# 80 gathered tokens instead of 48, every second chunk of expert rows in plain fp32, rows by 512 KB in eight slots

## The reference, cut to what matters

```
qry = (hc @ w_query).reshape(-1, PEER_HEADS, 2, PEER_HALF)
...
act = jax.nn.gelu(jnp.einsum('cd,chkd->chk', hc, expert_u[idx]))
return jnp.einsum('chk,chkd->cd', gate * act, expert_v[idx])
```

## Time and profile before

| what | us |
|---|---|
| median of three runs | 2206.61 |
| the profiled execution | 2206.82 |
| its span | 2205.1 |
| TensorE busy | 2182.6 |
| DVE busy | 1657.7 |
| ACT busy | 1216.1 |
| GpSimd busy | 688.0 |

### The profile page before, as it was taken

The page is one execution under the profiler, slowest core; times in us unless marked ns, Lnnn a source line. Parts: engine busy times, 40 slices in busy tenths (PEclk is TensorE's granted clock), DMA queues, the critical chain, the costliest instruction groups (busy, mean ns, idle before and its releaser), DMA issues.

```text
span 2205.1 us, 55760 instructions
## 1 busy us (share of the span) xinstructions
PE 2182.6 (99%) x16578; PEld 2138.2 (97%) x16578; DVE 1657.7 (75%) x3045; ACT 1216.1 (55%) x2220; POOL 688.0 (31%) x516
## 2 busy tenths in 40 slices
PE   9999999999999999999999999999999999999998
PEld 8999899999999999999999999999999999999997
DVE  8788778886766767888886444467788887888887
ACT  6445366667455444555555444454565565555664
POOL 0321100002011000788888888500454122111120
PEclk9999999999999999999999999999999999999999
DMA  7887756666556555777777888698899998788885
GB/s 241 288 292 246 240 185 213 203 213 220 183 190 207 175 165 185 187 182 183 189 178 183 194 186 182 161 333 282 278 315 300 304 316 299 274 293 299 297 284 188
DMA packets 337994, 514.37 MB, mean 233 GB/s; under 512 B 87276, under 2 KB 126564, under 8 KB 337772
## 3 DMA queue, kind: packets, MB, share of 16 engines
q1 hardware_dynamic: 263244, 427.59, 60.0%
q0 software_dynamic: 58016, 71.54, 13.0%
q10 hardware_dynamic: 16640, 14.16, 2.0%
HBM read 487.87 MB, written 25.24 MB: 233 GB/s over the span
## 4 chain that ended last, share of the span: by engine, by line
PE 75%; DMA 1%; DVE 1%; ACT 0%; issue 0%; SPq 0%; DVEq 0%; ACTq 0%
PE ps L2173 18%; PE ps L314 15%; PE ps L317 15%; PE ps L313 15%; PE ps L2177 10%; DMA raw<-expert_v 0%; DMA raw<-weights 0%; PE ps L2197 0%; PE ps L1400 0%; ACT hi L296 0%; DVE x L2154 0%; DVE lo L301 0%; PE ps L2206 0%; DVE x L2095 0%; DVE whl L2034 0%
## 5 line engine op out<-in xcount | busy, mean ns | idle before, releaser
L301 DVE TENSOR_TENSOR lo<-raw,hi 128x512 fp32r<-128x512 f32 x1504 | 1027.8, 695 | 462.9 <-ACT hi L296 435.1
L296 ACT CAST hi<-raw 128x512 fp32r<-128x512 f32 x1504 | 924.5, 620 | 720.7 <-PE ps L317 443.0
L313 PE MATMUL ps<-h_hi,hi 128*128 128x264 f32 (+1 forms) x3200 | 821.4, 286 | 2.7 <-DVE h_lo L954 2.7
L314 PE MATMUL ps<-h_lo,hi 128*128 128x264 f32 (+1 forms) x3200 | 820.2, 286 | 0.0
L313 PEld LDWEIGHTS ps<-h_hi,hi 128*128 128x128 f32 x3200 | 601.9, 188 | 10.2 <-issue 6.1
L314 PEld LDWEIGHTS ps<-h_lo,hi 128*128 128x128 f32 x3200 | 602.3, 188 | 0.0
L317 PE MATMUL ps<-h_hi,lo 128*128 128x264 f32 (+1 forms) x3200 | 523.4, 285 | 2.1 <-DVE lo L301 1.9
L1732 POOL DMA_INDIRECT w_spill<-chosen,widx x256 | 442.2, 1727 | 265.1 <-DVE widx L1956 187.0
L2173 PE MATMUL ps<-whl,hi 128*128 128x432 f32 x2048 | 489.7, 361 | 1.9 <-ACT half_sum L1817 1.2
L317 PEld LDWEIGHTS ps<-h_hi,lo 128*128 128x128 f32 x3200 | 444.4, 188 | 3.8 <-DVE lo L301 3.5
L2173 PEld LDWEIGHTS ps<-whl,hi 128*128 128x128 f32 x2048 | 348.8, 190 | 10.6 <-issue 1.7
(11 more groups left out here) (300 smaller groups left out, 1787.9 us busy)
## 6 DMA issues: line engine op xcount, KB each, us to landing
raw<-u_tiles SPq DMA_DIRECT2D x512, 256.0 KB
raw<-expert_v SPq DMA_DIRECT2D x512, 256.0 KB
raw<-weights SPq DMA_DIRECT2D x480, 256.0 KB
w_spill<-zeros ACTq DMA_DIRECT2D x16, 864.0 KB, 6.0
wld<-w_spill SPq DMA_DIRECT2D x32, 432.0 KB, 4.4
qb<-q_spill POOLq DMA_DIRECT2D x8, 512.0 KB, 6.3
w_spill<-chosen,widx POOLq DMA_INDIRECT x256
u_spill<-ust SPq DMA_DIRECT2D x128, 24.0 KB
```

What stands on the lines that cost most here:

```text
L296: nc.scalar.copy(hi[k % SPLIT][:], raw_quarter(k)).then_inc(hi_done, 1)
L301: nc.vector.tensor_tensor(lo[k % SPLIT][:], raw_quarter(k), hi[k % SPLIT][:].bitcast(F32), ALU.subtract).then_inc(lo_done, 1)
L313: pe.matmul(out, a, rhs[0][:, first + j, 0:n], start=start and j == 0, stop=False)
L314: pe.matmul(out, a, rhs[1][:, first + j, 0:n], start=False, stop=False)
```

## The change

The gathered tokens become 80, in groups of 16 and 64, so the dense columns fall from 216 to 184. DVE makes five additions per iteration of eight chunks (ADDS: in places k = 1, 2, 3, 5, 6; none in the first iteration of the first half, six in its iterations 8 to 12). Ten words are gathered first, then two after each row from row 2 on. Odd chunks, but for the first and the last of them, are native: TensorE multiplies their rows as loaded, in plain fp32, with W in plain fp32 (`plain`), and no engine splits them; `credit` lets the counters of splits pass over them. Rows come as whole chunks of 512 KB into eight slots; a slot is free when a split chunk's two parts are made, or when TensorE is through a native chunk. Chunks 4 to 7 wait for chunks 0 to 3, and the last spill of u now stands behind the load of chunk 7. TensorE's loop covers eight chunks; the loops of ACT and DVE are written out.

```
-GROUPS = (16, 32)
+GROUPS = (16, 64)
+NATIVE = (1, 3, 5, 7)
+SLOTS = 8
...
+    raw_v = place("raw_v", at["W"], [P, SLOTS - RAW, HALF, P])
+    wld = place("wld", at["raw_v"], [P, 3, 4, TD])
...
-    LATE_ADDS = [(0, 2, 4, 6), (0, 2, 4, 6), (0, 2, 4, 6), (0, 2, 4)]
-    BOUNDS = (0, 1, FIRST, 8, LATE)
-    assert 3 * (LATE - 1) + sum(len(a) for a in LATE_ADDS) == TG and 3 * (NK // 8) == TG and GROUPS == (16, 32)
+    BOUNDS = (1, 3, 6, 9)
+    FIVE, SIX = (1, 2, 3, 5, 6), (1, 2, 3, 5, 6, 7)
+    ADDS = [[()] + 7 * [FIVE] + 4 * [SIX] + [SIX, FIVE, FIVE, (0, 1, 2, 3, 4)], 15 * [FIVE] + [(0, 1, 2, 3, 4)]]
...
+    def column(n):
+
+        turn, m = n % TG // TURN, n % TURN
+        return GROUPS[0] + (TURN - 1) * turn + m if m < TURN - 1 else turn
...
+    def native(m):
+
+        return m % 8 in NATIVE and m not in (1, 2 * NK - 1)
...
+    def expert_slot(s):
+
+        return raw[:, s] if s < RAW else raw_v[:, s - RAW]
...
+    def expert_in(s):
+
+        return raw_in[s % RAW][s // RAW]
...
+    def credit(q):
+
+        return 3 if q % 2 and native(q // 2 + 1) else 1
+
+    def expert_hi(act, q):
+        wait_expert(act, q)
+        act.wait_ge(mm_done, 2 * C0 + q + 1)
+        nc.scalar.copy(hi[q % SPLIT][:], expert_quarter(q)).then_inc(hi_done, credit(q))
+
+    def expert_lo(dve, q):
+        dve.wait_ge(hi_done, 2 * C0 + q + 2 * RAW + 1)
+        dve.wait_ge(mm_done, 2 * C0 + q + 1)
+        nc.vector.tensor_tensor(lo[q % SPLIT][:], expert_quarter(q), hi[q % SPLIT][:].bitcast(F32),
+                                ALU.subtract).then_inc(lo_done, credit(q))
...
+            for i in range(NK // 8):
+                if p == 0 and i in BOUNDS:
+                    between(0, i, None)
                 for k in range(8):
-                    half(1, 0, k)
-                with eng.Fori(1, LATE) as i:
-                    for k in range(8):
-                        half(1, i, k)
-            for i in range(LATE, NK // 8):
-                for k in range(8):
-                    if p == 0 or i < NK // 8 - 1 or k < 6:
-                        half(p, i, k)
-                    elif k == 6:
-                        half(p, i, k, 1)
+                    m = NK * p + 8 * i + k
+                    for q in (2 * m + AHEAD, 2 * m + AHEAD + 1):
+                        if q < 4 * NK and split_chunk(q // 2):
+                            split(eng, q)
+                    if k % 2 == 0 and m + 2 < 2 * NK:
+                        w_part(m + 2)
+                    between(p, i, k)
...
+    def w_chunks(c):
+
+        return 2 if split_chunk(c + 1) else 1
...
-        load_half(sp, C0 + RAW, 0, expert_v[0, RAW])
+        def load_expert(p, i, s):
+            m = NK * p + 8 * i + s
+            first = isinstance(i, int) and p == 0 and i == 0
+            back = m - (RAW if first else SLOTS)
+            if native(back if isinstance(i, int) else s + SLOTS):
+                sp.wait_ge(mm_done, 2 * (C0 + back) + 2 + SPLIT)
+            else:
+                sp.wait_ge(hi_done, 2 * (C0 + back) + 2 + 2 * RAW)
+                sp.wait_ge(lo_done, 2 * (C0 + back) + 2 + 2 * RAW)
+            sp.dma_start(expert_slot(s).rearrange("p a b -> p (a b)"), expert_v[p, 8 * i + s]).then_inc(expert_in(s), 16)
+        for s in range(RAW, SLOTS):
+            load_expert(0, 0, s)
         spill(PAIR_U - 1, 1)
...
+        load_expert(0, 1, 0)
+        load_expert(0, 1, 1)
         sp.wait_ge(w_mul, UP_CHUNKS + 4)
         cells_in(UP_CHUNKS + 1, 1)
-        stream(2, 3)
+        for s in range(2, SLOTS):
+            load_expert(0, 1, s)
...
+        with sp.Fori(0, NK // 8) as i:
+            for s in range(SLOTS):
+                load_expert(1, i, s)
...
+        for n in range(FIRST_WORDS):
             gather_u(n)
-        words = WORD_TURNS[1]
+        words = FIRST_WORDS
...
+            n = w_chunks(c)
+            nc.scalar.copy(whl[c // 2 % 2][:, 0:n, 0], W[:, c % NK:c % NK + n, :]).then_inc(whi_done, 2)
...
+        def add_rows(n):
+            j, b = column(n), n % 3
+            g = 0 if j < GROUPS[0] else 1
+            dve.wait_ge(gat_in[b], 16 * (n // 3) + 16)
             dve.wait_ge(gat_used, n + 1)
-            nc.vector.scalar_tensor_tensor(out=gacc[:, g], in0=gat[b][:], scalar=gw[:, bass.ds(j, 1)],
+            nc.vector.scalar_tensor_tensor(out=gacc[:, g], in0=gat[b][:], scalar=gw[:, j:j + 1],
...
+                weigh_rows(BOUNDS.index(i))
...
+            if (i, k) in ADD_AT[p]:
+                n = TG * p + ADD_AT[p][i, k]
+                if n == TG:
                     dve.wait_ge(gacc_zero, 2)
-                add_rows(1 - m // 2, TG + 3 * i + m, column(i, m), m, i + TG // 3)
-            if p == 1 and static and i == LATE + 1 and k % 4 == 0:
+                add_rows(n)
...
+        def plain(p, i, k, r, stop):
+            if isinstance(i, int) and not p and not i and k < RAW:
+                pe.wait_ge(raw_in[k][r], 16 * PAIR_U + 16)
+            elif r == 0:
+                pe.wait_ge(expert_in(k), 16 * (PAIR_U + 1 + NK // SLOTS * p + (k >= RAW)) + 16 * i)
+            for j in range(QT):
+                m = pe.matmul(ps[:, bank(QT * r + j), 0:TD], expert_slot(k)[:, QT * r + j],
+                              W[:, 8 * i + k if isinstance(i, int) else bass.ds(8 * i + k, 1), :],
+                              start=False, stop=stop, skip_group_check=True)
+            m.then_inc(mm_done, 1)
+
+        def quarter(p, i, k, r, stop=False):
+            if native(NK * p + 8 * i + k if isinstance(i, int) else k + SLOTS):
+                plain(p, i, k, r, stop)
+            else:
+                first = isinstance(i, int) and i == 0 and k == 0
+                f(NK * p + 8 * i + k, k, r, first, stop, p == 1 and first)
         for p in range(2):
+            for k in range(8):
+                for r in range(2):
+                    quarter(p, 0, k, r)
+            with pe.Fori(1, NK // 8 - 1) as i:
+                for k in range(8):
+                    for r in range(2):
+                        quarter(p, i, k, r)
...
```

More of the change, by code:

```diff
@@ L116, in program @@
     sums = place("sums", at["wsum"], [P, 2, TT, PH])
-    gch = place("gch", at["sums"], [P, 3, TG])
-    gw = place("gw", at["gch"], [P, TG])
+    gw = place("gw", at["sums"], [P, TG])
     gu = place("gu", at["gw"], [P, TG])
@@ new lines, in program @@
+    ADDS = [[()] + 7 * [FIVE] + 4 * [SIX] + [SIX, FIVE, FIVE, (0, 1, 2, 3, 4)], 15 * [FIVE] + [(0, 1, 2, 3, 4)]]
+    TURN = TG // (NK // 8)
+    assert all(sum(len(a) for a in adds) == TG for adds in ADDS) and GROUPS == (NK // 8, (TURN - 1) * NK // 8)
+    ADD_AT = [{k: sum(len(a) for a in adds[:i]) + n for i in range(NK // 8) for n, k in enumerate([(i, k) for k in adds[i]])}
+              for adds in ADDS]
+    G_FIRST = [sum(GROUPS[:g]) for g in range(len(GROUPS))]
+    WORD_TURNS = [-(-sum(len(a) for a in ADDS[0][:i]) // TURN) * TURN for i in BOUNDS] + [TG]
@@ L1583, in gather_rows @@
     def gather_rows(n):
-        j = column(n % TG // 3, n % 3)
+        j = column(n)
         index = gidx[:, 1 + n // TG, j:j + 1]
@@ L1590, in halves @@
     def halves(eng, w_part, split, between, after_pass):
[L1592 to L1598, removed]
-        for p in range(2):
[L1600 to L1604, removed]
-                        for k in range(8):
-                            half(0, i, k)
-                between(0, None, None)
-            else:
-                for k in range(8):
-                    half(1, 0, k)
-                with eng.Fori(1, LATE) as i:
-                    for k in range(8):
-                        half(1, i, k)
-            for i in range(LATE, NK // 8):
-                for k in range(8):
-                    if p == 0 or i < NK // 8 - 1 or k < 6:
-                        half(p, i, k)
-                    elif k == 6:
-                        half(p, i, k, 1)
+        for p in range(2):
+            for i in range(NK // 8):
+                if p == 0 and i in BOUNDS:
+                    between(0, i, None)
+                for k in range(8):
+                    m = NK * p + 8 * i + k
[5 more added lines that the diff above has]
+                    between(p, i, k)
             after_pass(p)
-    def chunk(i, k):
-        n = 8 * i + k
-        return bass.ds(n % NK if isinstance(i, int) else n, 2)
+    def w_chunks(c):
+        return 2 if split_chunk(c + 1) else 1
     def experts_sync(sp):
@@ L1747, in gather_u @@
         def gather_u(n):
-            j, batch = column(n // 3, n % 3), max(b for b in range(4) if n >= WORD_TURNS[b])
+            j, batch = column(n), max(b for b in range(4) if n >= WORD_TURNS[b])
             nc.gpsimd.indirect_dma_start(gu[:, j:j + 1], None, u_rows,
```

115 lines of the change are left out of this document (46 added, 69 removed).

## The result

The change made the kernel slower by 0.28%: 2212.86 us (median of 20 runs, 2207.35 to 2219.07) against 2206.06 (median of 20, 2203.27 to 2209.92), ratio 1.0028, 95% interval 1.0021 to 1.0036. That is just over the 0.2% that can be told from no change. The forecast was 2198.5 us and faster; 2212.86 lies inside its range of 2186 to 2216, but on the other side of the kernel before. The profiled execution of the changed kernel took 2210.11 us with a span of 2208.3.

A forecast was written before the change was run, and what follows sets the result against it. The prediction took TensorE, busy for 99% of the span, to bound the kernel. Its terms -25.3, -2, +11, +7 and +1 summed to -8.3 us, from 2206.8 to 2198.5 us, range 2186 to 2216.

The forecast's parts named there:

- Part 1: TensorE's work per chunk: split chunks fall to 2.226 us, plain ones take 2.48, against 2.45 before; -25.3 us.
- Parts 2 and 5: Work off ACT and DVE, costed at nothing; buffer turns in six-addition iterations fit, last additions closer to the ends, +1 us.
- plain products at 0.457 ns: Rival on TensorE: plain products go at the rate of rounded ones, 2.69 us per plain chunk; 2217 us, chance 0.10.
- code fetched again: Rival: TensorE's loop of eight chunks fetches its code again at each jump back, +36 us; 2235 us, chance 0.08.
- a DMA bound: Rival: DMA becomes the bound, at 350 GB/s the second half takes 311 us instead of 301; 2206.5 us, chance 0.14.
- Part 3: SP's queue: the last spill issues late, so words and gw come late and TensorE waits near 1574; +11 us (8 to 14).
- the clock behind it: Lower TensorE clock after the stall near 1574: 2 to 3 us, costed at nothing because GpSimd's pace absorbs it.
- the rival that it costs nothing: Rival: the late spill costs nothing, if words are not what DVE waits for; 2188 us, chance 0.05.
- Part 4: GpSimd's pace: a row and two words take 3.98 us, five 19.9 against 18.8, over iterations 2 to 7; +7 us.
- the rival that GpSimd keeps pace: Rival: GpSimd issues words and rows at 1.24 us each and nothing is lost; 2190 us, chance 0.17.
- the pace term: The +7 us of Part 4, for GpSimd's issue of rows and words.

The follow-up runs named there:

- e13: Changed kernel with DVE's additions of gathered rows cut from 1024 to 128 elements per partition; 2197.45 us, 0.9937 of the kernel before.
- e1: Changed kernel with the last spill of u issued right behind the load of chunk 4, as before the change; 2209.94 us, 1.0004 of the kernel before.
- e2: Changed kernel with one and two words in turn behind each row, gw in five batches; 2205.96 us, 0.9984 of the kernel before.
- e3: Changed kernel with the early spill and the thinner words together; 2201.78 us, 0.9965 of the kernel before.
- e6: Changed kernel with a fourth buffer for gathered rows in the first half, nothing else; 2204.86 us, 0.9982 of the kernel before.
- e10: Changed kernel with the early spill and a fourth buffer, still two words behind each row; 0.9960 of the kernel before.
- e11: Changed kernel with early spill, thinner words, a fourth buffer and no plain chunk (all split); 1.0014 of the kernel before.
- e9: Changed kernel run again with nothing edited; 1.0024 of the kernel before.
- e7: Changed kernel with early spill, one and two words in turn, and a fourth buffer in the first half; 2192.01 us, 0.9926 of the kernel before.

## Why the prediction was wrong, point by point

**Part 1, TensorE's work: right in kind, too large.** -19.8 us instead of -25.3. The split chunk takes 2.24 us (2.226 predicted), the plain one 2.505 (2.48). The plain rate of 0.421 ns was right to 1%. Four low products go at 0.42 us (0.44 before) with 15% fewer columns, so they gained next to nothing, as assumed; the four high ones gained some 0.08 us per quarter instead of 0.112.

**Parts 2 and 5: right.** No row load was late for TensorE, and the second half had no wait at all. The rivals of plain products at 0.457 ns, of code fetched again (61 packets on the instruction queue, 56 before, and no wait of TensorE at any jump back) and of a DMA bound fell: from 1900 to 2160 the kernel moved 360 GB/s, and TensorE was busy for all of the 260 us. (The 397 GB/s that the prediction asks of an iteration with six additions doesn't follow from its other numbers: 14 transfers of 524 KB in 18.8 us come to 390.) Of the two rules of the Trainium skill that the prediction weighed, neither showed. The limit of about 358 GB/s ("DMA: Bandwidth & Descriptors", Specifications) was passed here and, with 387 GB/s, from 1750 to 1860. A loop of 256 products and weight loads jumped back without a stall; the section that the prediction cites for it ("Runtime: NRT & Kernel Launch", Instruction fetch mechanics) gives TensorE's instruction store as 2048 instructions, so that its rule was weak ground for a rival here.

**Part 3, the late spill: right**, and the rival that it costs nothing fell. SP's timeline and DVE's:

```profile
1547.60 11.71 SPq L1735 DMA_DIRECT2D raw_v<-expert_v  x4
1559.36 0.42 SPq L1665 DMA_DIRECT2D u_spill<-ust  x1
```

```profile
1581.65 0.24 DVE L2092 TENSOR_TENSOR gw<-gu,gch 128x2 f32<-128x2 f32 x2 [13.05 <-DMA gu<-u_spill,gidx]
```

The spill went out at 1559.36 (1560.7 predicted, 1550.68 before), DVE's gw came at 1581.65, and TensorE lost 10.1 us (11 predicted). What the prediction costed at nothing was the clock behind it:

```profile
1576.60:1583.00 6.40, 0.00 (x0) 0.00 (x0) 1.32 (x5) 0.00 (x0) 4.73 (x5) 0.50 0.97 323
1583.00:1586.90 3.90, 3.88 (x15) 3.88 (x16) 2.51 (x4) 0.86 (x2) 0.83 (x1) 0.51 1.02 415
1586.90:1590.00 3.10, 3.10 (x22) 3.10 (x22) 3.10 (x5) 0.62 (x1) 2.49 (x3) 1.00 0.88 312
```

From 1583.0 to 1586.9 TensorE worked at 1.2 GHz, 1.7 us lost by the step it was in. The reason given (GpSimd's pace runs on meanwhile and absorbs it) failed, as the next term accrues later.

**Part 4, GpSimd's pace: the step that failed.** It was named, placed and bounded rightly, and mis-sized: 16.2 us instead of 7. The pace taken was the calm row, 3.98 us; 4.28 came, and over seven and a half iterations instead of six. That the crowded row of 4.27, which the same part named with +15 us, comes so close is a coincidence: its two long issues stood behind a split and a product of W with the gates, not behind an addition. The ground for the choice, that DVE's splits halve and so GpSimd runs as in the calm part, left out DVE's additions. With this term falls the rival that GpSimd keeps pace. GpSimd in the changed kernel, and DVE beside it:

```profile
1598.43 1.96 POOL L1639 DMA_INDIRECT gat<-expert_v,gidx  x1 [0.30 <-issue]
1600.69 0.95 POOL L1790 DMA_INDIRECT gu<-u_spill,gidx  x1 [0.31 <-issue]
1601.94 0.94 POOL L1790 DMA_INDIRECT gu<-u_spill,gidx  x1 [0.30 <-issue]
1603.19 1.81 POOL L1639 DMA_INDIRECT gat<-expert_v,gidx  x1 [0.30 <-issue]
```

```profile
1598.28 1.28 DVE L2085 SCALAR_TENSOR_TENSOR gacc<-gat,gw,gacc 128x1024 f32<-128x1024 f32 x1 [0.98 <-DMA gat<-expert_v,gidx]
...
1602.91 1.28 DVE L2085 SCALAR_TENSOR_TENSOR gacc<-gat,gw,gacc 128x1024 f32<-128x1024 f32 x1
```

Both long issues began inside an addition and ended some 0.82 us behind its end: 1598.43 + 1.96 = 1600.39 against 1599.56, and 1605.00 against 1604.19. So did each of the 12 issues over 1.5 us between 1590 and 1733. DVE's other operations with two inputs do the same: of the 100 issues begun there, 44 began inside an addition (22), a split (14) or an operation on W (8) with over 0.15 us of it left, and all 44 ended 0.81 to 0.83 us behind its end; 55 of the other 56 took 0.94 to 0.96 us. Of the 18.1 us that the 100 took beyond 0.944 each, 13.0 belong to additions. Issues that had begun first, as one at 1606.56 (1.05 us) ahead of an addition from 1606.71 to 1607.99, were not held up by it. e13 is the run that shows the cause. The Trainium skill, "SBUF — State Buffer", section "SBUF: two separate sides", has the rule: a DVE operation with two inputs from SBUF holds a port that it shares with GpSimd for its whole length, and a GpSimd operation that reads SBUF waits. The trace agrees for the gathers, which wait when they begin second. It doesn't show the other direction: the 23 additions that began inside an issue took 1.28 to 1.29 us like the rest.

The rows that the prediction read don't show an addition's price, and that is the lesson of the case: GpSimd then waited for DVE's addition before nearly every row, so a row was issued just *behind* an addition. But the trace of the kernel before held the price. Of the 73 issues begun from 1550 to 1720 there, 45 began inside a split or an operation on W and ended 0.82 us behind it, and one, a word, met an addition and took 2.01 us (GpSimd, then DVE):

```profile
1589.78 2.01 POOL L1749 DMA_INDIRECT gu<-u_spill,gidx  x1 [0.30 <-issue]
```

```profile
1589.70 1.27 DVE L2040 SCALAR_TENSOR_TENSOR gacc<-gat,gw,gacc 128x1024 f32<-128x1024 f32 x1
```

Beyond 3.72 us, a row with two words took 0.39 us for splits and operations on W and 0.04 for additions before, 0.15 and 0.39 in the changed kernel. The first part fell, as the prediction had it; the second came as soon as GpSimd waits for nobody and additions fall anywhere on its issues. The prediction carried a duration over from a state that the change itself ended.

**The sum.** -25.3, -2, +11, +7, +1 became -19.8, -3, +10.1 and +1.7 of clock, +16.2, 0. Against the forecast of -8.3 the pace term is off by 9 us, TensorE's work by 5.5, the clock by 1.7. That makes +5.2, of which the spans show 3.2 (the stage began 1.2 us earlier). The medians stand 6.8 us apart, because the profiled execution of the changed kernel is quicker than its median by 2.75 us and that of the kernel before slower than its own by 0.76; which waits are longer in a median run of the changed kernel is not shown. That the measured time still lies inside the forecast's range is no merit of the sum: the range held GpSimd's slowest pace.

## What to carry to other kernels

Before an engine's pace is carried over, ask what that engine waited for when it was measured: a wait that aligns it with another engine's work also hides most of what the two do to each other. Build the new price from the issue that met nothing and from what each kind of overlap adds, and look for the one overlap of each kind that the trace may already hold. A gather engine that also feeds a stream of small gathers needs slack over TensorE's time per iteration; here one word less behind every second row was worth 10 us, half of what all the removed multiplications gave. And when loads move ahead in a queue, look at the one small transfer behind them that somebody else's first step needs: one line moved back was worth 4 to 5 us in each of three pairs of runs (the changed kernel and e1, e2 and e3, e6 and e10).

## What the runs showed of the hardware that was not expected

**GpSimd's issue time follows what DVE is doing.** The second half, 1900 to 2160 us, in the changed kernel and without plain chunks (e11), DVE busy being the third figure of each first line:

```profile
1900.00:2160.00 260.00, 260.00 (x1756) 260.00 (x1755) 174.85 (x237) 87.08 (x181) 70.06 (x68) 1.00 0.97 360
...
L1639 POOL DMA_INDIRECT gat<-expert_v,gidx x68 | 70.1, 1030 | 189.1 <-DVE gacc L2085 181.5 <-issue 7.6
```

```profile
1900.00:2160.00 260.00, 249.95 (x1719) 245.37 (x1718) 241.14 (x339) 159.90 (x285) 126.72 (x68) 0.98 0.97 354
...
L1644 POOL DMA_INDIRECT gat<-expert_v,gidx x68 | 126.9, 1866 | 133.9 <-DVE gacc L2091 133.3 <-issue 0.6
```

The same 68 row gathers take 1.03 us with DVE busy for 67% of the time and 1.87 us with 93%. In the changed kernel 38 of them met nothing (0.94 us) and 29 began inside a split (1.14 to 1.26). In e11 66 began inside a split, and only half of them took 1.15 us; the others took 1.74 to 7.46, while DVE went on from operation to operation.

**Some short waits cost clock, others don't.** The long stalls near 1573 were followed by the lower level every time (0.50 or 0.51 in the changed kernel, e2, e6, e9 and e13); of the waits of about 2 us some were (2.16 us in e1, 2.61 and 2.26 in e9) and some not (1.78 in the changed kernel, 2.73 in e1). Kernels with many waits spread more from run to run: the changed kernel over 11.7 us in 20 runs, at mean clocks of 0.996 to 0.991 (of the five slowest four at 0.991 or 0.992, of the five quickest none under 0.993), e11 over 23 us in 12, and e7, with few waits, over 2 us in 5. That the clock makes the spread is likely but was not tested by itself.
